# Rotary turn as a VectorE lane shuffle with GpSimd arithmetic, and modulation weights loaded from SyncE's queue

## The reference

```python
def modulate(x, shift, scale):
    return x * (1.0 + scale[:, None, :]) + shift[:, None, :]
def partial_rotary(t, pos):
    half = ROT_DIM // 2
    ...
    t1, t2 = tr[..., :half], tr[..., half:]
    rot = jnp.concatenate([t1 * cos - t2 * sin, t2 * cos + t1 * sin], axis=-1).astype(t.dtype)
    return jnp.concatenate([rot, t[..., ROT_DIM:]], axis=-1)
...
        mod = (cond @ w_ada[l] + b_ada[l]).reshape(b, 3 * N_SUB, d)
        h = modulate(x, mod[:, 0], mod[:, 1])
        x = post_norm_residual(x, swiglu(h, w_ffn_in[l, 0], w_ffn_out[l, 0]), mod[:, 2], 0.5, ln_g[l, 0], ln_b[l, 0])
        h = modulate(x, mod[:, 3], mod[:, 4])
        if l < N_A_LAYERS:
            q, k, v = jnp.split(h @ w_qkv_a[l], 3, axis=-1)
            q = partial_rotary(split_heads(q), pos)
            k = partial_rotary(split_heads(k), pos)
```

## Time and profile before

| | |
|---|---|
| median of 3 runs | 1090.98 us |
| lowest and highest | 1090.12, 1091.12 us |
| span of the profiled execution | 1088.1 us |
| PE busy | 1052.3 us, 97% of the span |
| DVE busy | 785.8 us, 72% |
| ACT busy | 515.5 us, 47% |
| POOL busy | 54.9 us, 5% |
| moved by DMA | 265.76 MB, mean 244 GB/s |
| granted TensorE clock, mean | 0.997 |

### The profile page before, as it was taken

The page is one execution under the profiler, slowest core; times in us unless marked ns, Lnnn a source line. Parts: engine busy times, 40 slices in busy tenths (PEclk is TensorE's granted clock), DMA queues, the critical chain, the costliest instruction groups (busy, mean ns, idle before and its releaser), DMA issues.

```text
span 1088.1 us, 18522 instructions
## 1 busy us (share of the span) xinstructions
PE 1052.3 (97%) x7269; PEld 959.2 (88%) x7279; DVE 785.8 (72%) x869; ACT 515.5 (47%) x822; POOL 54.9 (5%) x82
## 2 busy tenths in 40 slices
PE   3999999999999999999999999999999999999996
PEld 1799999978898899999979999999979779999995
DVE  7687778789864886768785577777789676544576
ACT  1644543463464644543464554444455664444333
POOL 0000001100000000001100001000100000000000
PEclk9999999999999999999999999999999999999999
DMA  9999999948744399999948399999967537665631
GB/s 358 325 345 351 323 314 291 353 148 267 275 117 120 105 306 310 297 314 290 348 151 232 118 297 291 300 310 288 333 228 231 195 87 223 193 192 170 186 147 39
DMA packets 248730, 265.76 MB, mean 244 GB/s; under 512 B 7273, under 2 KB 212457, under 8 KB 248681
## 3 DMA queue, kind: packets, MB, share of 16 engines
q1 hardware_dynamic: 226848, 183.13, 55.1%
q0 software_dynamic: 19776, 75.53, 19.4%
q10 hardware_dynamic: 2056, 6.42, 1.7%
HBM read 264.01 MB, written 1.05 MB: 244 GB/s over the span
## 4 chain that ended last, share of the span: by engine, by line
PE 92%; DVE 3%; ACT 3%; DMA 1%; issue 1%; DVEq 0%; SPq 0%
PE psum L1081 20%; PE psum L1082 20%; PE psum L1083 20%; PE psum L1189 9%; PE psum L1190 9%; PE psum L1191 9%; PE psum L1120 1%; PE psum L1128 1%; PE psum L1308 1%; DMA raw<-in_w_ada 1%; DVE tmp L734 1%; DVE acc L734 1%; PE psum L1111 1%; ACT tmp L478 1%; ACT h_full L478 1%; PE psum L1261 1%
## 5 line engine op out<-in xcount | busy, mean ns | idle before, releaser
L1081 PE MATMUL psum<-hT_hi,w_hi 128*128 128x256 f32 x1664 | 475.5, 286 | 2.9 <-DVE hT_lo L833 1.7
L1083 PE MATMUL psum<-hT_hi,w_lo 128*128 128x256 f32 x1664 | 471.6, 283 | 0.0
L1082 PE MATMUL psum<-hT_lo,w_hi 128*128 128x256 f32 x1664 | 471.5, 283 | 0.0
L702 DVE TENSOR_TENSOR w_lo<-raw,w_hi 128x2048 fp32r<-128x2048 f32 x164 | 375.2, 2288 | 125.6 <-ACT w_hi L408 125.6
L408 ACT ACTIVATE w_hi<-raw 128x2048 fp32r<-128x2048 f32 x164 | 313.0, 1909 | 111.0 <-PE psum L1191 109.8
L1081 PEld LDWEIGHTS psum<-hT_hi,w_hi 128*128 128x128 f32 x1664 | 319.0, 192 | 13.7 <-issue 4.3
L1082 PEld LDWEIGHTS psum<-hT_lo,w_hi 128*128 128x128 f32 x1664 | 319.1, 192 | 1.0
L1083 PEld LDWEIGHTS psum<-hT_hi,w_lo 128*128 128x128 f32 x1664 | 319.0, 192 | 0.0
L734 DVE SCALAR_TENSOR_TENSOR acc<-ada,cond,acc 128x1024 f32<-128x1024 f32 x130 | 166.6, 1282 | 9.3 <-DMA ada<-in_w_ada 5.8
L413 ACT ACTIVATE tmp<-psum 128x256 f32<-128x256 f32 x88 | 33.7, 383 | 278.4 <-PE psum L1083 278.4
L1189 PE MATMUL psum<-w_hi,a_hi 128*128 128x512 f32 x352 | 139.2, 396 | 0.0
(11 more groups left out here) (154 smaller groups left out, 837.3 us busy)
## 6 DMA issues: line engine op xcount, KB each, us to landing
raw<-in_w_ffn_in SPq DMA_DIRECT2D x176, 512.0 KB, 6.0
ada<-in_w_ada POOLq DMA_DIRECT2D x64, 1024.0 KB, 5.7
raw<-in_w_ffn_out SPq DMA_DIRECT2D x88, 512.0 KB, 5.2
raw<-in_w_qkv_a SPq DMA_DIRECT2D x24, 512.0 KB, 6.5
raw<-in_w_o SPq DMA_DIRECT2D x16, 512.0 KB, 5.6
ada<-in_w_kv_ada POOLq DMA_DIRECT2D x8, 1024.0 KB, 6.2
raw<-in_w_kv_b SPq DMA_DIRECT2D x16, 512.0 KB, 6.4
raw<-in_w_ada SPq DMA_DIRECT2D x6, 1024.0 KB, 11.0
```

Source lines behind the costliest of these rows:

```text
L702: nc.vector.tensor_tensor(w_lo[:, n % SPL, :], raw[:, n % RAW, :], w_hi[:, n % SPL, :].bitcast(F32), ALU.subtract).then_inc(w_lo_ready, 1)
L1081: nc.tensor.matmul(dst, s_hi, m_hi, start=start, stop=False)
L1082: nc.tensor.matmul(dst, s_hi, m_lo, start=False, stop=False)
L1083: return nc.tensor.matmul(dst, s_lo, m_hi, start=False, stop=stop)
```

## The change

The matrix `rot_m` goes, its 128 columns of constants too, and the sign moves into the table of sines. VectorE exchanges the two halves of 16 rows with one `stream_shuffle` from `qT`/`kT` into a buffer in SBUF (two in turn, in `h_full` and `tmp`). GpSimd then multiplies that buffer by the sines, the rows by the cosines, waits for both, and adds. GpSimd issues no loads any more. SyncE issues the loads of the modulation weights between the pairs of raw chunks: a table `taken` says how many quarters VectorE has consumed by the time that the low half of a chunk is made, and behind the load of chunk n (`refill`) come the quarters whose buffers are free by chunk n - 6. SyncE's loops are written out for that.

```diff
+        taken = {}
+        for f in range(4):
+            steps = [(1 + 2 * b + i, ((1, 1, 0))) for b in range(LOOPS) for i in range(2)] if FIRST_UNIT[f] is not None else []
+            for s, counts in steps + [(STEPS - 2, (2, 1, 1))]:
+                for i in range(3):
+                    taken[N_FFN[f] + 3 * s + 2 + i] = counts[i]
...
         @block.sync
...
+            def load_quarter(u, q):
...
+                sp.wait_ge(acc_steps, 8 * u + 2 * q - 2)
+                sp.dma_start(ada[:, q % 2, :, :], ada_view(w)[:, 2 * q:2 * q + 2, j * D:(j + 1) * D])\
+                    .then_inc(ada_in[q % 2], 16)
+
+            def refill(n):
+
+                done = 4 * (STAGED // 4) + sum(c for m, c in taken.items() if m <= n - RAW)
+                while filled[0] < min(done + 2, 4 * UNITS):
+                    load_quarter(filled[0] // 4, filled[0] % 4)
+                    filled[0] += 1
...
             load_wo(1)
             load_ffn(3)
+            refill(N_ALL + RAW)
...
         @block.gpsimd
...
-            for u in range(STAGED // 4, UNITS):
-                load_unit(u)
+            def rope(i):
+
+                own_half = (qT, kT)[i // 4][0:ROT, 2 * (i % 4):2 * (i % 4) + 2, :]
+                other = swapped[i % 2].rearrange("p (h t) -> p h t", h=2)
+                two = [ROT, 2, SEQ]
+                pool.wait_ge(swap_ready, i + 1)
+                nc.gpsimd.tensor_tensor(other, other, sin_t.unsqueeze(1).to_broadcast(two), ALU.mult)\
+                  .then_inc(rope_step, 1)
+                nc.gpsimd.tensor_tensor(own_half, own_half, cos_t.unsqueeze(1).to_broadcast(two), ALU.mult)\
+                  .then_inc(rope_step, 1)
+                pool.wait_ge(rope_step, 2 * i + 2)
+                nc.gpsimd.tensor_tensor(own_half, own_half, other, ALU.add).then_inc(rope_done, 1)
...
+            def swap_halves(i):
+
+                dve.wait_ge(proj_kept, i + 1)
+                if i >= 2:
+
+                    dve.wait_ge(rope_done, i - 1)
+                nc.vector.stream_shuffle(swapped[i % 2].rearrange("p (h t) -> p h t", h=2),
+                                         (qT, kT)[i // 4][0:ROT, 2 * (i % 4):2 * (i % 4) + 2, :], SWAPPED)\
+                  .then_inc(swap_ready, 1)
...
-                    rope(i - 1)
+                    swap_halves(i - 1)
...
+            swap_halves(7)
             for i in range(4):
                 soft_max(2 * i)
                 soft_max(2 * i + 1)
-                if i == 0:
-
-                    rope(7)
...
-            rotate(0)
             for i in range(2, 8):
                 pe.wait_ge(proj_kept, i - 1)
                 columns_out(N_QKV + i, gu[i % 2])
-                rotate(i - 1)
```

More of the change, by code:

```diff
@@ L110 @@
 GATE_W = [0.5, 1.0, 0.5, 0.5, 1.0, 0.5]
-C_ID, C_TRI, C_CAUSAL, C_STRICT, C_KEEP, C_COS, C_SIN, C_ROT = (
-    0, 128, 256, 384, 512, 640, 896, 1152)
-C_ALL = 1280
+C_ID, C_TRI, C_CAUSAL, C_STRICT, C_KEEP, C_COS, C_SIN = (
+    0, 128, 256, 384, 512, 640, 896)
+C_ALL = 1152
+SWAPPED = [(i + ROT // 2) % ROT for i in range(ROT)]
 NORM_OF_FFN = [0, 2, 3, 5]
@@ L243, in build @@
         proj_kept = sem("proj_kept")
-        rot_ready = sem("rot_ready")
+        swap_ready = sem("swap_ready")
+        rope_step = sem("rope_step")
         rope_done = sem("rope_done")
@@ L294, in build, with load @@
                 [(N_Q + i, w_q_b[0], 256 * i) for i in range(4)])
+        taken = {}
[4 more added lines that the diff above has]
+                    taken[N_FFN[f] + 3 * s + 2 + i] = counts[i]
+        for i in range(2, 6):
+            taken[N_QKV + i + 3] = 1
+        taken[N_Q + 4] = 2
+        taken[N_WO[1] + 1] = 2
         @block.sync
         def _(sp):
-            def load(n, halves, at=None):
-                if at is not None or n >= RAW:
-                    sp.wait_ge(w_lo_ready, n - RAW + 1 if at is None else at + (n - RAW + 1))
+            filled = [4 * (STAGED // 4)]
+            def load_quarter(u, q):
+                layer, j = ORDER[u]
+                w, b = (w_kv_ada, b_kv_ada) if layer == KV else (w_ada[layer], b_ada[layer])
+                if u in GATE_OF and q == 0:
+                    g = GATE_OF.index(u)
+                    if g:
+                        sp.wait_ge(acc_steps, 8 * GATE_OF[g - 1] + 1)
+                    else:
+                        sp.wait_ge(set_up, 1)
+                    sp.dma_start(bias0[0:1, :], b[j * D:(j + 1) * D].rearrange("(a n) -> a n", a=1))\
+                        .then_inc(bias_in, 16)
+                sp.wait_ge(acc_steps, 8 * u + 2 * q - 2)
[6 more added lines that the diff above has]
+                    filled[0] += 1
+            def load(n, halves):
+                if n >= RAW:
+                    sp.wait_ge(w_lo_ready, n - RAW + 1)
                 else:
@@ L320, in load_ffn @@
                 load(n + 1, inner_chunk(w_in, P))
-                peeled = 2 if f == 0 else 0
-                for s in range(1, 1 + peeled):
+                for s in range(1, STEPS):
                     load_step(w_in, w_out, n, s)
[L325 to L330, removed]
+                    if f == 0 and s == 2:
+                        sp.dma_start(cst[:, P:], consts[:, P:]).then_inc(cst_in, 16)
                 load(n + FFN_CHUNKS - 1, rows_chunk(w_out, DFF - 256))
@@ L1347, in _ @@
                 scores(2 * i + 1)
-                if i == 0:
-                    rotate(7)
                 values_out(i)
@@ L1442, in shape_constants @@
         a[i * half:(i + 1) * half, C_COS:C_COS + SEQ] = np.cos(angle)
-        a[i * half:(i + 1) * half, C_SIN:C_SIN + SEQ] = np.sin(angle)
-    for i in range(half):
-        a[i + half, C_ROT + i] = -1.0
-        a[i, C_ROT + i + half] = 1.0
+        a[i * half:(i + 1) * half, C_SIN:C_SIN + SEQ] = np.sin(angle) * (1.0 if i else -1.0)
     return a
```

53 lines of the change are left out of this document (10 added, 43 removed).

## The result

The changed kernel takes **1118.76 us** (median of 4 runs, 1116.05 to 1120.46) where the kernel before took 1090.82 in the same session: ratio 1.0257, 95% interval 1.0245 to 1.027. The forecast, 1100.4 with a range up to 1107.0, had the sign and about a third of the size.

A forecast was written before the change was run, and what follows sets the result against it. TensorE, busy 97% of the span, was taken to bound the kernel. Terms -9.9 + 12.4 + 0.8 + 6.1 = +9.4 us on the 1088.1 us span gave 1097.5, plus 2.9 around it 1100.4 us; range 1091.0 to 1107.0.

The forecast's parts named there:

- I cost GpSimd's last turns at nothing: Attention softmax: GpSimd's last rotary turns add no time, because the value chunk (5.8 us) covers them.
- the raw pair taken at its issue time of before: Gate steps: the raw pair ahead of quarter 2 is issued as in the old trace, at 204.92 and 780.79.
- quarter 2's landing: Gate steps: pair in 5.0 us after its issue, quarter 3.0 us more, so landing 8.0 us after the pair's issue.
- the start of the first FFN at nothing: FFN loops, first included: a few microseconds of later issue are covered, quarters being needed 17 us after their buffer frees.
- The turns' removal from PE, -9.9 us: First projection: eight rotary turns leave PE, 1.24 us a chunk each, none of it hidden; -9.9 us in all.
- The gate steps, +12.4 us: Gate ends of three FFNs: quarter 2 lands late behind the raw pair, PE waits 4.1 to 4.2 us each; +12.4 us.
- FFN loops at nothing: Inside FFN loops: a quarter is needed 17 us after its buffer comes free, so later issue is covered; no cost.
- Layer 1's query projection, +0.8: Layer 1's query projection: quarter 2 comes 2.3 us late, 1.2 absorbed by DVE's idle time; +0.8 us (0 to 2.3).
- The fourth FFN at nothing: Fourth FFN's gate: no chunk left to load behind, SyncE waits directly for the accumulation; no cost.
- GpSimd's arithmetic, +6.1 us up to the first scores: First projection: DVE and GpSimd take turns, 1.0 us per GpSimd operation; scores at 291.8 instead of 285.7, +6.1 us.
- such a wait in the softmax: Sign of being wrong: a PE wait that none of the terms has, above all in the softmax.
- The third rival's case: Modulation loads: quarter 2 does not queue behind the raw pair, landing within 7.1 us of its issue; 1088.4 us, chance 0.13.

The follow-up runs named there:

- Few columns: Changed kernel with each quarter issued one raw chunk earlier, GpSimd's products and sum on only 8 of 256 columns, the other columns' turn left out: 1080.42 us, ratio 0.9912.
- held clock: Changed kernel with 21 products of zeros on PE ahead of chunk 30 in three FFNs, where PE is idle: 1113.27 us, ratio 1.0213.
- early in the loops only: Changed kernel with only the quarters that follow FFN-loop chunks, a gate's quarter 1 among them, issued one chunk earlier: 1116.69 us, ratio 1.0237.
- Early issue: Changed kernel with each quarter issued one raw chunk earlier, ahead of the raw pair it stood behind: 1091.03 us, ratio 1.0006.
- turn alone: Changed kernel with all modulation loads issued by GpSimd, those of the projection between its turns: 1093.34 us, ratio 1.0025.

## Why the prediction was wrong

**What failed, in short.** 9.4 us were forecast and 30.5 measured, span against span. The largest step that failed is one that the sum makes without saying it: that PE's work takes as long behind a wait as it did before (a chunk 5.76 us). The lower clock behind PE's waits cost 6.6 us in the gate steps and 3.8 in the attention, about half of what is missing. The other failed steps are "I cost GpSimd's last turns at nothing" (7.6 us, with those 3.8), the raw pair taken at its issue time of before, without quarter 1 (3.6 us), quarter 2's landing (2.2 us) and the start of the first FFN at nothing (1.5 us).

**The turns' removal from PE, -9.9 us: right.** "Few columns" measured 9.9 in the stage, and its first scores start at 285.8 where 285.7 was predicted.

**The gate steps, +12.4 us: the mechanism right, the size half.** They measured 24.8. The waits were 18.2 us in three (20.1 less 1.9 in the projection), not 12.4. The clock added 6.6: every one of these waits was followed by a chunk of 7.3 to 8.4 us, "held clock" showed that it is the clock, and no row shown had PE idle in the middle of the program.

Of the waits' 5.8 us too many, "early in the loops only" tells two parts. With quarter 1 in time the three waits were 14.6 us (16.5 less 1.9). So 2.2 us belong to "The quarter is 1.05 MB more; at the 348 GB/s of the stretch after 204.92 that is 3.0 us", put on a pair in at 5.0: quarter 2 landed 8.5 to 8.7 us after the pair's issue (208.40 to 217.04 in the first FFN), not 8.0. The other 3.6 us belong to the pair, which was taken at the issue times of before. In the first FFN it came 3.5 us later, 1.5 of them from the start of the program and 2.0 because DVE waited for quarter 1, which is behind a pair as well. That quarter was not costed at all.

**FFN loops at nothing: nearly right.** The cover of 17 us held in all of them but the first turns, where an issue took up to 3.95 us: +1.5. "Early issue" has none of it.

**Layer 1's query projection, +0.8: measured +1.2.** The fourth FFN at nothing: measured 0.0.

**GpSimd's arithmetic, +6.1 us up to the first scores: right, in part by luck.** From the gate's broadcast to the first scores the change takes 71.5 us and "few columns" 66.3, so 5.2 were measured. From the first shuffle to the fifth turn's end 39.0 us were predicted (252.8 to 291.8) and 37.9 measured (263.79 to 301.68). An operation took 1.27 us alone, not 1.0, but it holds DVE up for 1.09 only: five splits of 2.29, four quarters of 2.59 and fifteen times 1.09 are 38.2 us. The 1.0 that I took and half a split too many came to the same. The rule that the prediction took from the Trainium skill (SBUF — State Buffer, Who interferes with whom) is borne out on both sides: two-input splits go from 2.29 to 3.38 beside GpSimd's reads and stay at 2.29 beside its writes, which the same section states; and of GpSimd's operations it is the reading ones that wait (2.26 us for one of 0.21). From a figure of the GPSIMD Engine Reference of the Trainium skill, section 3.1, I had estimated 1.12 us an operation; the trace has 1.27 alone and 1.09 of hindrance.

**The last turns at nothing "because the value chunk (5.8 us) covers them": wrong, and the failed step of this half.** It costs 7.6 us: from first scores to gate broadcast 44.0 instead of 36.3 ("few columns": 322.13 - 285.81). I looked for GpSimd's lateness at PE, in the scores. Half of it (3.9 us) is PE waiting for the softmax. It came through DVE's order: the last shuffle waits for GpSimd's sixth turn, and the softmax of the first heads is queued behind it; and the softmax's own operations of one input are slowed to 1.2 us. This is read off the chain; no run moves the last shuffle alone. The other half (3.8 us) is the clock, behind these waits and the one for the first scores. The prediction itself had named such a wait in the softmax as the sign that it was wrong. The stage has +3.0 where -3.8 was predicted.

Together: -3.8, +12.4 and +0.8 were 9.4; measured were +3.0, +24.8, +1.2 and +1.5, 30.5. Two small things in the prediction's sums decide nothing: the runs on record are 1.8 to 1.9 us longer than their spans, not 2.9, so the same sum would give about 1099.4; and the ends of the range are, by their own terms, 1091.3 and 1107.2.

The third rival's case (a landing within 7.1 us of the pair's issue) did not come in any run of this queue order; the landings were 8.5 to 9.5 us behind it. What stays open: why quarter 2 behind its pair takes 8.6 us and not 8.0, and why GpSimd's turn costs 11.0 us in "early issue", 12.9 in the change and 13.5 in "turn alone". PE's busy time in the stage is 101.8, 103.4 and 104.4 us in the three, so most of the difference is the same work done at the lower clock; why the waits fell so that the clock was low for longer is not shown.

## What to carry over

When a load moves to another queue, look not at the queue but at the event that now releases it: one raw chunk earlier or later was 28 us here, while the queue itself was worth nothing. Where PE has to wait, add to the wait what the chunk behind it will take at the lower clock; here a wait of 5 to 7 us cost 1.6 to 2.6 more. And work given to GpSimd beside a VectorE that is nearly full costs both engines: the same three operations cost less on VectorE itself (3 x 0.68 us) than taking turns with GpSimd at 1.27 us each, and whoever waits for GpSimd in VectorE's order passes that wait to all behind.

## What the runs showed of the hardware

- A split with two SBUF inputs takes 2.29 us and 3.38 beside a product or sum of GpSimd that reads 32x512 elements from SBUF (+1.09); a pair of accumulations 2.59 and 3.9. Beside GpSimd's memsets they take 2.29 and about 2.6.
- It works the other way too: a product of GpSimd on 32x16 elements took 0.21 us alone and 2.26 when it started beside a split; a memset of 32x512 took 0.52 in either case.
- The granted clock fell to its lower level behind five waits of PE in the change, of 2.9 to 6.9 us. The three chunks behind the gates' waits took 1.6 to 2.6 us longer by it.
- One-input operations from SBUF to SBUF are hit too, and harder in proportion: a negated maximum of 128x2 elements went from 0.17 to 1.13 us, a scaling of 128x256 from 0.35 to 1.37. The reductions from PSUM beside them (0.26 and 0.40 us) were not.
- The shuffle of 32x512 elements takes 0.72 us, with its mask's load 0.01, against 0.68 for a product of that shape: I had taken 0.68.
- A DMA issue of SyncE takes 0.4 to 0.5 us later in the program, and at its start, while the first loads are under way, up to 3.95 us (6.16 in "early issue").
- A megabyte quarter lands 6.2 us after its issue in "early issue", 7.7 right behind a pair (209.36), and 10.9 between two pairs (192.61).
